# A second feed-forward product turned around: each Strassen product runs over all pairs of hidden blocks in PSUM, and VectorE splits its operands

## The reference

```python
for i in range(DEPTH):                      # 2 layers, 1024 tokens, D_MODEL 1024, D_FF 4096
    ...                                     # a mixer, then layer norm
    hid = jnp.square(jax.nn.relu(jnp.einsum('bsd,df->bsf', x, ffn_w1[i])))
    x = layer_norm(DEEPNORM_ALPHA * x + jnp.einsum('bsf,fd->bsd', hid, ffn_w2[i]), ln2_g[i], ln2_b[i])
    gate = jax.nn.sigmoid(jnp.einsum('bsd,de->bse', x, ple_gate_w[i]))
    x = x + gate * jnp.einsum('bsk,kd->bsd', p[i], ple_w[i])
```

## Time and profile before

| | us |
|---|---|
| median of three runs (2134.71 to 2137.01) | 2134.86 |
| the profiled execution | 2136.69 |
| its span, first to last instruction | 2134.9 |
| PE busy in the span | 2115.5 |
| the second product of layer 0, with its wide stages | from about 575 to 892 |
| the same of layer 1 | from about 1690 to 2007 |

### The profile page before, as it was taken

The page is one execution under the profiler, slowest core; times in us unless marked ns, Lnnn a source line. Parts: engine busy times, 40 slices in busy tenths (PEclk is TensorE's granted clock), DMA queues, the critical chain, the costliest instruction groups (busy, mean ns, idle before and its releaser), DMA issues.

```text
span 2134.9 us, 28066 instructions
## 1 busy us (share of the span) xinstructions
PE 2115.5 (99%) x10613; PEld 1796.4 (84%) x10613; DVE 1396.5 (65%) x1991; ACT 776.6 (36%) x1185; POOL 992.4 (46%) x597
## 2 busy tenths in 40 slices
PE   9999999999999999999999999999999999999999
PEld 9887788888878888899888888888888878888899
DVE  5744775556698888675543353676555798788774
ACT  3112455444543333521211101554445533333521
POOL 5113167777655546112422223258877655556120
PEclk9999999999999999999999999999999999999999
DMA  5111124434655443201121111024444664443211
GB/s 184 40 60 51 29 80 153 153 138 154 209 201 177 138 168 99 79 26 45 40 79 40 60 40 55 25 87 155 157 154 144 211 200 165 138 168 104 65 38 72
DMA packets 150018, 233.87 MB, mean 110 GB/s; under 512 B 11169, under 2 KB 80893, under 8 KB 149885
## 3 DMA queue, kind: packets, MB, share of 16 engines
q1 hardware_dynamic: 149184, 231.78, 32.6%
...
## 4 chain that ended last, share of the span: by engine, by line
PE 88%; DVE 6%; POOL 2%; issue 2%; ACT 1%; DVEq 0%; ACTq 0%; POOLq 0%
PE bank_a L1763 15%; PE bank_a L1765 15%; PE bank_a L1764 15%; PE bank_b L1763 14%; PE bank_b L1765 14%; PE bank_b L1764 14%; POOL op_lo L942 1%; PE bank_a L1802 1%; DVE resid L1520 1%; DVE xt_lo L1314 1%; POOL op_sum L1015 1%; PE bank_b L1802 1%; DVE xt_hi L1309 1%; DVE resid L1551 0%; PE bank_a L1978 0%
## 5 line engine op out<-in xcount | busy, mean ns | idle before, releaser
L927 POOL TENSOR_TENSOR w_lo<-raw,w_hi 128x512 fp32r<-128x512 f32 x160 | 223.4, 1426 | 674.8 <-ACT w_hi L1036 674.7
L1763 PE MATMUL bank_a<-xt_hi,w_hi 128*128 128x512 f32 x640 | 251.4, 393 | 2.7 <-DVE xt_lo L1314 2.7
L1765 PE MATMUL bank_a<-xt_hi,w_lo 128*128 128x512 f32 x640 | 249.2, 389 | 0.0
L1764 PE MATMUL bank_a<-xt_lo,w_hi 128*128 128x512 f32 x640 | 249.1, 389 | 0.0
L969 POOL TENSOR_TENSOR wop_lo<-w_sum,wop_hi 128x1024 fp32r<-128x1024 f32 x56 | 135.3, 2416 | 231.7 <-ACT wop_hi L1143 231.7
L1763 PE MATMUL bank_b<-w_hi,xt_hi 128*128 128x256 f32 x640 | 182.7, 285 | 2.7 <-DVE xt_lo L1314 2.3
L1036 ACT CAST w_hi<-raw 128x512 fp32r<-128x512 f32 x160 | 88.3, 620 | 255.8 <-PE bank_a L1765 154.7
L1765 PE MATMUL bank_b<-w_hi,xt_lo 128*128 128x256 f32 x640 | 181.1, 283 | 0.0
L1764 PE MATMUL bank_b<-w_lo,xt_hi 128*128 128x256 f32 x640 | 181.1, 283 | 0.0
L1763 PE MATMUL bank_b<-wop_hi,hop_hi 128*128 128x512 f32 x464 | 180.8, 390 | 0.0
L1765 PE MATMUL bank_b<-wop_hi,hop_lo 128*128 128x512 f32 x464 | 180.6, 389 | 0.0
(11 more groups left out here) (188 smaller groups left out, 5364.8 us busy)
## 6 DMA issues: line engine op xcount, KB each, us to landing
h_raw<-h_spill SPq DMA_DIRECT2D x106, 512.0 KB, 3.7
...
w_raw<-in_ffn_w_dram SPq DMA_DIRECT2D x64, 512.0 KB, 5.4
w_raw<-in_ffn_w_dram SPq DMA_DIRECT2D x112, 256.0 KB, 3.5
...
```

The lines of the kernel that those rows point to most:

```text
L927: pool.tensor_tensor(w_lo[slab % 2][:, s], raw[:, n % NRAW, :], w_hi[slab % 2][:, s].bitcast(F32), ALU.subtract).then_inc(lo_split, 1)
L1763: pe.matmul(dst, s_hi, m_hi, start=first, stop=False, skip_group_check=on_top)
L1764: pe.matmul(dst, s_hi, m_lo, start=False, stop=False, skip_group_check=on_top)
L1765: return pe.matmul(dst, s_lo, m_hi, start=False, stop=last, skip_group_check=on_top)
```

## The change

- `PAIRS` is 8: blocks 0 and 1 are a pair too, the last that each product takes (`pair`). The wide stages, `common`, the fold and `w_sum` go.
- `ITEMS` is turned around. A product ("form") now runs over all eight pairs, item after item, into the same four banks, and is flushed once (L1527 or L1530 of the changed kernel). The order is m1 for the pairs 1 to 7 and 0 (items 0 to 7); then m6 and m2 in turn (items 8 to 23); then m5, m3, m7 and m4, eight items each (24 to 55). m6, m5, m3 and m4 accumulate onto what an earlier form left in the banks.
- m6 follows m1 in the banks a0 to a3: its first group waits until m1's flush has read the bank.
- Each item loads its own weight quarters, in 512 KB pieces with 2 KB rows: three for m6, one for the others, 72 in all. The sum that m5, m7 and m4 use again stays in SBUF (`t2_of`).
- DVE makes all low parts of the 56 items, and the sums. POOL has nothing in this product.
- Roles 4, 2, 5 and 6 of the first pair were never made by the trips. The stages psum_in, psum and psum_out make them: SP loads four 512 KB quarters, DVE adds four times, SP stores four results.
- Operands live in five slots: item n takes the slot of item n - 5 (the last eight by a table), so its cast waits until PE has finished that item.
- The layer norm of tokens 0 to 511 and their transposes lie among the items from 40 on. The last two items are fused, tile by tile.

```diff
+FORMS = dict(m1=("A", 0, ("b11",), 0), m6=("A", 5, ("b12", "b11", "b22"), 2), m5=("A", 4, ("b22",), 1),
+             m3=("A", 6, ("b22",), 0), m2=("B", 1, ("b21",), 0), m7=("B", 2, ("b11",), 1), m4=("B", 3, ("b21",), 1))
+ITEMS = ([("m1", j) for j in range(PAIRS)] + [(form, j) for j in range(PAIRS) for form in ("m6", "m2")]
+         + [(form, j) for form in ("m5", "m3", "m7", "m4") for j in range(PAIRS)])
+LAST_SLOTS = (3, 4, 0, 1, 3, 4, 0, 3)
...
@@ make_plan
+        for i, (form, j) in enumerate(ITEMS):
+            while i and nxt < len(ITEMS) and (a.user_before(nxt) is None or a.user_before(nxt) < i):
+                prepare(layer, nxt)
+                nxt += 1
+            st = add("prod", item=i, layer=layer, head=heads.get(form))
...
+            if i in (1, 2, 3):
+                add(("psum_in", "psum", "psum_out")[i - 1], layer=layer)
...
+    def prepare(layer, n):
+        if n + 1 < len(ITEMS):
+            add("wsum", item=n + 1, layer=layer)
+        add("prep", item=n, layer=layer)
...
@@ SP
+            def load_item(layer, i):
+                if a.hop_before(i) is not None:
+                    sp.wait_ge(ahead_dve, a.hop_low[a.hop_before(i)])
...
+                sp.dma_start(h_raw[a.hop_chunk(i)][:, :, :], src).then_inc(h_in[slot], 16)
+                for n, quarter in enumerate(FORMS[form][2]):
...
+                    if before is not None:
+                        sp.wait_ge(ahead_dve, a.w_user(before))
...
+                    sp.dma_start(w2_raw[a.w_chunk(load)][:, :, :], rows[:, :, f, :]).then_inc(w2_in[slot], 16)
+                if st.kind == "prep" and st.item >= 4 and st.item + 4 < len(ITEMS):
+                    load_item(st.layer, st.item + 4)
...
@@ POOL
-                    if o not in H_LOW_DVE:
-                        pool.tensor_tensor(hop_lo[k][:, :, :], h_raw[a.load(i)[0]][:, :, :],
-                                           hop_hi[k][:, :, :].bitcast(F32), ALU.subtract).then_inc(ahead_pool, 1)
...
@@ DVE
+                if st.kind == "psum":
+                    dve.wait_ge(first_in, 64 * (st.layer + 1))
+                    dve.tensor_tensor(c22, c12, c22, ALU.add).then_inc(first_step, 1)
...
+                if st.kind == "prep":
+                    dve.wait_ge(ahead_hi, a.act[i] - 1)
+                    dve.tensor_tensor(hop_lo[k][:, :, :], h_raw[a.hop_chunk(i)][:, :, :],
+                                      hop_hi[k][:, :, :].bitcast(F32), ALU.subtract).then_inc(ahead_dve, 1)
+                    dve.wait_ge(ahead_hi, a.act[i])
+                    dve.tensor_tensor(wop_lo[k][:, :, :], w2_source(a, i), wop_hi[k][:, :, :].bitcast(F32),
+                                      ALU.subtract).then_inc(ahead_dve, 1)
+                if st.kind == "prod" and ITEMS[st.item][1] == PAIRS - 1:
...
@@ PE
+                        if ITEMS[i][1] == 0:
+                            dst = free_bank(ring, st, k)[:, :]
...
+                            for q in range(2):
+                                ins = product(dst, (hop_hi[s][:, q, t], hop_lo[s][:, q, t]),
+                                              (wop_hi[s][:, q, :], wop_lo[s][:, q, :]), q == 0 and j == 0 and not on_top,
+                                              q == 1 and j == PAIRS - 1, on_top)
```

More of the change, by code:

```diff
@@ L168, in load @@
-    def load(self, i):
-        s = i % 4
-        per_layer = len(range(s, PIECES_PER_LAYER, 4))
-        return s, 16 * (self.layer * per_layer + i // 4 + 1)
-    def block_load(self, b):
-        return b % 2, 32 * (self.layer * (PAIRS + 1) // 2 + b // 2 + 1)
+        n = len(ITEMS)
+        self.act = [2 * n * layer + 2 * i + 2 for i in range(n)]
+        self.first_load = [sum(len(FORMS[form][2]) for form, _ in ITEMS[:i]) for i in range(n)]
+        self.loads = sum(len(FORMS[form][2]) for form, _ in ITEMS)
@@ new lines, in __init__ @@
+        sums, taken, dve = sum(FORMS[form][3] for form, _ in ITEMS), 0, 0
+        dve = layer * (2 * n + sums)
+        self.sum, self.hop_low, self.dve, self.taken = [None] * n, [], [], []
+        for i in range(-1, n):
+            if i + 1 < n:
+                dve += FORMS[ITEMS[i + 1][0]][3]
+                self.sum[i + 1] = dve
+            if i >= 0:
+                self.hop_low.append(dve + 1)
+                dve += 2
+                self.dve.append(dve)
+                taken += ITEMS[i][1] < PAIRS - 1 and i != n - 2
+                self.taken.append(layer * (len(FORMS) * (PAIRS - 1) - 1) + taken)
@@ L187, in spilled, with w_user, w_before @@
+    def w_user(self, load):
+        i = max(i for i in range(len(ITEMS)) if self.first_load[i] <= load)
+        if ITEMS[i][0] == "m6":
+            return self.sum[i]
+        return self.dve[i]
+    def w_before(self, load):
+        return next((k for k in range(load - 1, -1, -1) if self.w_chunk(k) == self.w_chunk(load)), None)
     def spilled(self, role, blk):
@@ L239, in make_plan @@
     trips = [Trips(layer) for layer in range(2)]
+    ahead = [Ahead(layer) for layer in range(2)]
     need = dict(xu=[0, 0], hu=[0, 0])
@@ L494, in trunk @@
     ahead = [Ahead(layer) for layer in range(2)]
+    heads = [{ITEMS[st.item][0]: st for st in plan if st.kind == "prod" and st.layer == layer and st.head is None}
+             for layer in range(2)]
     n_slabs = total["slab"]
@@ L867, in stage @@
                             spill(layer, b, 6, h_tile[6])
-                        if op == "A22" and b == last:
-                            sp.wait_ge(trip_done, tr.done[b, op])
-                            load_w2(layer, 1, (0,))
                 if st.kind == "lasthid":
@@ L1104, in stage @@
                 if st.kind == "second":
-                    for name, value in ends[st.layer]["full"][-2:]:
-                        act.wait_ge(sem_of[name], value)
+                    act.wait_ge(ahead_dve, ahead[st.layer].dve[-1])
                     split_high(st.cur + 2, st.piece + 5, 4)
+                    split_high(st.cur + 2, st.piece + 9, 1, at=4)
                 if st.kind == "consts":
@@ L1131, in stage @@
+                    k, form = a.slot(i), ITEMS[i][0]
+                    if a.user_before(i) is not None:
+                        name, value = item_done(a, a.user_before(i))
                         act.wait_ge(sem_of[name], value)
                     else:
-                        act.wait_ge(ahead_pool, a.pool[n * PAIRS - 1])
-                    slot, landed = a.load(i)
+                        act.wait_ge(trip_done, trips[st.layer].done[FFN_BLOCKS - 1, ("S1", "S2", "A12", "S4", "A22")[i]])
```

500 lines of the change are left out of this document (213 added, 287 removed).

## The result

| | before | after |
|---|---|---|
| median, us (runs) | 2135.94 (4) | 2187.27 (4) |
| lowest to highest | 2134.71 to 2137.11 | 2185.58 to 2188.05 |
| span of the profiled execution | 2134.9 | 2185.0 |

What follows compares the result with a forecast made beforehand. PE was taken as the bound, busy 99% with 88% of the chain. Terms: -17.4 + 2 x (10.8 + 14.6) + 3.1 + 3.0 = +39.5 on 2136.69, 2176.2, or 2174 against the median; range 2144 to 2200, the forecast's own 2165 to 2186.

Steps and rivals of the forecast that it cites:

- B: Rival: the queue is less full than assumed, so both waits vanish under PE's lead; -14.4 us, 2120; chance 0.14.
- D: Rival: only the wait before item 7 comes, m1's flush being in time; +10.3 us, 2145; chance 0.12.
- E: Rival: no change in time, needing waits of some 4 us each for items 7 and 8; chance 0.02.
- First wait: PE waits 10.8 us a layer before item 7, whose low parts stand behind the first pair's additions on DVE.
- The chunk: DMA queue: a 512 KB chunk takes 1.37 us, from 383 GB/s; bounds 1.27 and 1.52, 1.75 as a rival.
- from there on the queue is never empty: First wait: after c21's spill leaves at 587.7, 20.5 chunks follow without a break, 28.1 us, landed at 616.9.
- Second wait: PE waits 14.6 us a layer before item 8 for m1's flush, behind sums on DVE that wait for load 12.
- Clock: PE falls to 1.2 GHz during the waits; the second wait costs 1.54 us in each layer, +3.1.
- Tail: End of product: PE waits 1.5 us a layer at the transposes, the gate's weight casts preceding ACT's squares; +3.0.
- Saved: PE in both layers: fewer matmuls -10.9, gaps gone -5.0, half clock in layer 1 gone -1.5; together -17.4 us.
- rival C: Slower still: the queue stays near 300 GB/s with stores and loads mixed; +62.5 us, 2197; chance 0.12.
- DVE at 1.14 us: DVE's low parts and sums take 1.14 us each with POOL idle here; the other end was 2.10.

Runs made afterwards that it cites:

- e1_late: Changed kernel with the first pair's loads, additions and stores placed behind items 8, 9 and 10 instead of 1, 2 and 3; 2159.02 us.
- e2_flush: Changed kernel with m1's flush on DVE ahead of item 12's sums and item 11's low parts; 2159.98 us.
- e4_stores: Changed kernel with the first pair's four stores behind load 12 on SP instead of ahead of it; 2177.68 us.
- e7_tail: e6_halves with the last bank's flush on DVE ahead of the `p` tiles at the product's end; 2119.71 us.
- e6_halves: Changed kernel with the first pair in two halves, loads two places ahead of the additions, and m1's flush behind item 8's low parts; 2125.41 us.
- e8_pool: e7_tail, but POOL instead of DVE makes 43 `hop_lo` low parts a layer (items 5 to 47); 2120.66 us.
- e3_both: Changed kernel with the edits of e1_late and e2_flush together; 2158.30 us.
- e9_early: e3_both with m1's flush moved behind item 8's low parts, as in e6_halves; 2162.93 us.

## Why the prediction was right, and where its sizes were off

The forecast of 2174 lies 13 us below the measured 2187.27, inside its range of 2144 to 2200 and just above the forecast's own upper end of 2186.

- **Both long waits, right in place, releaser and cause**, and shown by experiment: e1_late removes the first, e2_flush all but 1.5 us of the second, e4_stores takes 5 to 7 us off the second. Rivals B (both hidden), D (only the first) and E (no change) fell.
- **First wait: 10.8 forecast, 13.3 and 12.2 measured** beyond pitch. The chunk was right: 385 to 396 GB/s, 1.32 to 1.36 us. So was DVE's part, 9.4 us against 9.5 from 619.33 to 628.85. The term "from there on the queue is never empty" failed: from 588 to 598 the queue moved 302 GB/s in place of 383, which is 2.1 us, and the quarters were there at 619.33 in place of 616.9.
- **Second wait: 14.6 forecast.** Counted as the forecast counts, from item 7's start and less 5.44, it is 16.1 and 15.8 (the paths are 21.5 and 21.2 us against 20.0). The queue had run dry, so load 11 paid the start of a lone transfer, which the working left out: load 12 was there 16.0 us after item 7 was ready, against 14.8.
- **Clock: 3.1 forecast, 5.5 measured.** I took the 1.54 us of the earlier trace rows for the second wait of each layer. Behind 14.3 us the half clock lasted 5.7 us and cost 2.7. The wait of 1.81 us in the earlier trace rows should have warned me, for it cost nothing: eight distances, to the row of 620.08 in the kernel before, took 1.90 us against 1.81 at pitch. That the first wait's clock falls into the second one was right. Between item 7's start and item 8's DVE works without a pause to 638 and then waits for load 12, whatever PE does; the slow matmuls of item 7 shorten PE's idle time, not this path. That is why PE's timeline above has 1.7 us as clock and 14.4 as wait, together the 16.1. In e2_flush, where the second wait is gone, the slow clock of item 7 does count (2.8 and 2.9 us).

```profile
620.08 0.39 PE L1765 MATMUL bank_a<-wop_hi,hop_lo 128*128 128x512 f32 x1
```

- **Tail: 3.0 forecast, 5.2 measured, and the mechanism was another.** The forecast put the wait down to the casts, ending 1.7 us after PE's last matmul. They ended at 918.24, 0.7 us before it (918.96). What was missed is in DVE's order: the last bank stood behind the `p` tiles, which wait for ACT, so that the last square started at 925.57. e7_tail moves that one step, leaves the casts, and the wait is gone. That a wait of a few us came there was right, its cause was not.
- **Saved: -17.4, nearly right**: 18.6 by what is left over above. e6_halves, where the waits are gone and the tail is not, stands 11.6 us under before; -17.4 and the tail's 5.2 make -12.2.
- **The rival C** (300 GB/s with stores and loads mixed) did not come: from 630 to 640, with the first pair's stores and the loads behind them in the queue, it moved 341 GB/s, and 391 from 640 to 650. The Trainium skill ("DMA: Bandwidth & Descriptors", Where 436 GB/s comes from) has HBM bind transfers to SBUF at about 358 GB/s. The traces don't agree: 391 here, and 395 and 413 in the earlier trace rows before.
- **DVE at 1.14 us, right**, which e8_pool shows from the other side.

In the forecast's own terms, both layers together, the first wait is short by 3.8 us, the second by 2.7, the clock by 2.4 and the tail by 2.2; the net saving is 0.5 larger than forecast. That makes 50.1 in place of 39.5. All four costs were set too low, so the forecast did not come near by errors that cancel. Of the 13 us to the median, the remaining 2.7 come from the way from one execution to the median (1.8 taken off for the kernel before, 0.6 for the changed one) and from rounding.

What I had not weighed was the remedy: the same three stages seven places later only move the wait to the reuse of their memory (e3_both, e9_early, a small part in e1_late). What stays open is what sets the length of the slow stretch. The length of PE's rest alone doesn't: 2.9 us were lost behind 4.7 idle microseconds (e9_early) and 1.7 behind 13.1.
